# One MoE transformer layer on one core: slots of an expert's block spread over the DMA engines, and no GpSimd drain at the end

## What is computed

```python
scores = sigmoid(t @ w_router); biased = scores + router_bias        # 64 experts
idx = top 8 experts out of the best 4 of 8 groups                    # per token
wsel = scores[idx] / sum(scores[idx]) * 2.5
routed[token] = sum over its 8 experts e of wsel * swiglu(t, wg[e], wu[e], wd[e])
swiglu(t, wg, wu, wd) = (silu(t @ wg) * (t @ wu)) @ wd               # 1024 -> 256 -> 1024
x = x + g2 * (routed + shared)
```

## Time and profile before

| | us |
|---|---|
| median of 3 runs | 1282.87 (1282.39 to 1285.67) |
| the profiled execution | 1285.91 |
| its span, first to last instruction | 1284.1 |
| PE busy | 1203.1 (94%) |
| DVE busy | 462.0 (36%) |
| ACT busy | 197.6 (15%) |
| POOL busy | 193.3 (15%) |

### The profile page before, as it was taken

How to read it: one execution, slowest core, us unless ns; L and a number is a source line. 1 busy time by engine, 2 the same in 40 slices (tenths; PEclk the granted TensorE clock), 3 DMA queues, 4 the chain that set the end, 5 groups by cost and what they waited for, 6 DMA issues and landing times.

```text
span 1284.1 us, 14047 instructions
## 1 busy us (share of the span) xinstructions
PE 1203.1 (94%) x4705; PEld 606.4 (47%) x4705; DVE 462.0 (36%) x1239; ACT 197.6 (15%) x452; POOL 193.3 (15%) x221
## 2 busy tenths in 40 slices
PE   6999999999999999998899998889999898999985
PEld 3444544444888544444444444333444343444442
DVE  2536557100666222555233323222323232233322
ACT  4110001011665001120001100000100010011100
POOL 0000000000221000100022323222222112223212
PEclk9999999999999999998899999988999899999998
DMA  8966661112100302167789999999999999989952
GB/s 275 368 217 229 219 231 65 66 65 83 50 0 1 131 1 106 72 256 290 278 294 364 383 386 378 382 364 375 370 300 379 386 363 391 384 291 381 358 135 35
DMA packets 88910, 311.52 MB, mean 243 GB/s; under 512 B 12400, under 2 KB 38160, under 8 KB 64912
## 3 DMA queue, kind: packets, MB, share of 16 engines
q1 hardware_dynamic: 72480, 272.77, 55.0%
q0 software_dynamic: 14784, 35.68, 11.8%
q10 hardware_dynamic: 1584, 2.27, 0.5%
HBM read 295.47 MB, written 34.08 MB: 257 GB/s over the span
## 4 chain that ended last, share of the span: by engine, by line
PE 80%; DMA 14%; DVE 2%; issue 1%; SPq 1%; ACT 1%; POOL 0%; DVEq 0%; POOLq 0%; ACTq 0%
PE PS L1718 21%; PE PS L1429 19%; PE PS L1739 11%; DMA R_HSA<-w_up_e 5%; DMA R_Z<-w_up_e 5%; PE PS L1597 4%; PE PS L1568 4%; PE PS L1704 3%; PE PS L1501 3%; PE PS L1477 2%; PE PS L1412 2%; DMA out<-second_sum 2%; DMA R_G<-h_rows,gidx 2%; PE PS L1607 2%; PE PS L1489 1%
## 5 line engine op out<-in xcount | busy, mean ns | idle before, releaser
L1429 PE MATMUL PS<-R_WT,R_HSA 128*128 128x512 f32 x576 | 248.2, 592 | 0.0
L1429 PEld LDWEIGHTS PS<-R_WT,R_HSA 128*128 128x128 f32 x576 | 109.3, 190 | 135.9 <-issue 135.8
L1265 DVE TENSOR_TENSOR R_G<-R_G,PS 128x256 f32<-128x256 f32 x50 | 30.4, 608 | 356.6 <-ACT R_G L864 356.6
L1718 PE MATMUL PS<-R_Z,R_G 128*64 128x512 f32 (+1 forms) x384 | 137.5, 603 | 13.0 <-DMA R_XM<-w_up_e 9.7
L1718 PE MATMUL PS<-R_WT,R_G 128*64 128x512 f32 (+1 forms) x352 | 129.1, 636 | 18.9 <-DMA R_WT<-w_up_e 10.9
L657 POOL DMA_INDIRECT R_G<-h_rows,gidx x54 | 56.3, 1042 | 431.6 <-DVE gidx L1254 370.5
L869 ACT ACTIVATE R_G<-PS 128x256 f32<-128x256 f32 x50 | 19.2, 383 | 556.2 <-PE PS L1726 556.2
L1286 DVE SCALAR_TENSOR_TENSOR R_G<-PS,slx,R_XM 128x512 f32<-128x512 f32 x100 | 74.9, 750 | 64.5 <-PE PS L1739 64.5
L1718 PEld LDWEIGHTS PS<-R_Z,R_G 128*64 128x64 f32 (+1 forms) x384 | 52.6, 161 | 92.9 <-issue 92.9
L1718 PE MATMUL PS<-R_XM,R_G 128*128 128x512 f32 (+1 forms) x192 | 88.0, 613 | 0.0
L1718 PEld LDWEIGHTS PS<-R_WT,R_G 128*64 128x64 f32 (+1 forms) x352 | 46.2, 163 | 84.7 <-issue 84.7
(11 more groups left out here) (256 smaller groups left out, 1318.6 us busy)
## 6 DMA issues: line engine op xcount, KB each, us to landing
R_Z<-w_gate_e SPq DMA_DIRECT2D x22, 1024.0 KB, 17.2
R_Z<-w_up_e SPq DMA_DIRECT2D x22, 1024.0 KB, 27.7
R_Z<-w_down_e SPq DMA_DIRECT2D x22, 1024.0 KB, 24.9
R_WT<-w_gate_e SPq DMA_DIRECT2D x21, 1024.0 KB, 16.6
R_WT<-w_up_e SPq DMA_DIRECT2D x21, 1024.0 KB, 30.1
R_WT<-w_down_e SPq DMA_DIRECT2D x21, 1024.0 KB, 27.1
R_WT<-ada_w SPq DMA_DIRECT2D x18, 1024.0 KB, 7.5
R_WT<-w_in SPq DMA_DIRECT2D x9, 2048.0 KB, 10.3
```

What stands on the lines that cost most here:

```text
L1265: dve.tensor_tensor(AR[:, b, :].rearrange("p (k d) -> p d k", k=2), by_line(SIL[:, b, :], 2), by_line(PS[:, b, F:2 * F], 2), ALU.mult).the ...
L1429: ins = mm(PS[:, t, :], HT[:, k, P * t:P * t + P], WR[:, b, k, :], start=k == 0, stop=k == KD - 1)
L1718: ins = mm(PS[w * h:w * h + w, b, :].rearrange("p (g n) -> p g n", g=2), XT[:, b, k, w * h:w * h + w], WGU[n][:, k], start=k == 0, stop=k ...
```

## The change

- `spread_slots(rows, turned)` numbers the slots anew: the partitions of a transfer are taken as 16 runs of rows/16, and neighbouring slots lie on different runs: slots 1 to 16 are the first partition of each run, 17 to 32 the second, and so on; turned, it goes through the runs from the last to the first. There are tables for 128, 96 and 64 rows, in both directions.
- Wide and narrow blocks use them turned at every other block; in a pair block the second expert is turned.
- The tables for 128 and 96 rows are a new input `slots` (128 x 448 float32, 224 KiB), loaded at the head of the shared weights' transfers; TensorE's wait counts one transfer more, and VectorE gets a wait for it ahead of the first `onehot`. For 64 rows the place of `C_SLOT` is used.
- In narrow blocks `onehot` compares 96 slots instead of 128.
- The block is opened with `no_gpsimd_drain=True`: GpSimd's drain at the end is left out.

```diff
+def spread_slots(rows, turned):
+    row = np.arange(rows)
+    engine = row // (rows // 16)
+    return row % (rows // 16) * 16 + (15 - engine if turned else engine) + 1
...
-    c[:, C_SLOT:C_SLOT + P] = f + 1
+    slots = np.zeros((P, S_N), np.float32)
+    for turned in range(2):
+        c[:, C_SLOT + P // 2 * turned:C_SLOT + P // 2 * turned + P // 2] = spread_slots(P // 2, turned)
+        slots[:, S_WIDE[turned]:S_WIDE[turned] + P] = spread_slots(P, turned)
+        slots[:, S_NARROW[turned]:S_NARROW[turned] + NARROW] = spread_slots(NARROW, turned)
...
+        SLOTS = R_T[:, 4096:4096 + S_N]
...
-        block = st.enter_context(nc.Block())
+        block = st.enter_context(nc.Block(no_gpsimd_drain=True))
...
+        def turned(j, b):
+            return (j - PAIRS[j]) % 2 if isinstance(j, int) and j < NM else b
...
             sp.wait_ge(s_u, 8)
+            sp.dma_start(SLOTS, a["slots"]).then_inc(s_ws, 16)
             sp.dma_start(R_W[:, 6144:6656], a["w_router"].rearrange("(p k) n -> p (k n)", p=P)).then_inc(s_ws, 16)
...
-                    dve.tensor_tensor(AH[:, b], bc(cst[:, C_SLOT:C_SLOT + P].unsqueeze(1), [P, NT, P]),
+                    n = rows(j)
+                    at = (S_WIDE if n == P else S_NARROW)[turned(j, b)]
+                    dve.tensor_tensor(AH[:, b, :, 0:n], bc(SLOTS[:, at:at + n].unsqueeze(1), [P, NT, n]),
...
-                                      bc(cst[:, C_SLOT:C_SLOT + h].unsqueeze(1).unsqueeze(1), [P, NT, 2, h]),
+                                      bc(cst[:, C_SLOT:C_SLOT + P].rearrange("p (c s) -> p c s", c=2).unsqueeze(1),
+                                         [P, NT, 2, h]),
...
+            dve.wait_ge(s_ws, 80)
             onehot(0, 0)
...
-            pe.wait_ge(s_ws, 64)
+            pe.wait_ge(s_ws, 80)
```

More of the change, by code:

```diff
@@ L123 @@
 C_N = C_SEL + HA
+S_WIDE = (0, P)
+S_NARROW = (2 * P, 2 * P + NARROW)
+S_N = 2 * P + 2 * NARROW
+def spread_slots(rows, turned):
+    row = np.arange(rows)
+    engine = row // (rows // 16)
+    return row % (rows // 16) * 16 + (15 - engine if turned else engine) + 1
 def constants():
@@ L157, in constants @@
     causal[:, S - P:] = np.where(f > p, NEG, 0.0)
-    return c, causal
+    return c, causal, slots
 def build(nc, a):
@@ L1222, in onehot @@
                 if len(cols) == 1:
-                    dve.tensor_tensor(AH[:, b], bc(cst[:, C_SLOT:C_SLOT + P].unsqueeze(1), [P, NT, P]),
+                    n = rows(j)
+                    at = (S_WIDE if n == P else S_NARROW)[turned(j, b)]
+                    dve.tensor_tensor(AH[:, b, :, 0:n], bc(SLOTS[:, at:at + n].unsqueeze(1), [P, NT, n]),
                                       bc(PM[:, bass.ds(cols[0], 1), :].rearrange("p o t -> p (o t)").unsqueeze(2),
-                                         [P, NT, P]), ALU.is_equal).then_inc(s_ah, 1)
+                                         [P, NT, n]), ALU.is_equal).then_inc(s_ah, 1)
                 else:
@@ L1801 @@
         give(name, array if name == "c" else array.reshape(array.shape[1:]))
-    for name, array in zip(("consts", "causal"), constants()):
+    for name, array in zip(("consts", "causal", "slots"), constants()):
         give(name, array)
```

## The result

| | before | after |
|---|---|---|
| median, us | 1284.27 (1280.37 to 1289.3, 6 runs) | 1276.72 (1273.09 to 1281.64, 6 runs) |
| profiled execution, its span | 1285.91, 1284.1 | 1281.64, 1279.8 |
| second comparison | 1285.12 (17 runs) | 1272.67 (1269.41 to 1276.35, 6 runs) |

The ratio is 0.9939, 95% interval 0.9918 to 0.9960, and in the second comparison 0.9906 (0.9877 to 0.9934). The change makes the kernel 0.6 to 0.9% faster, 8 to 12 us where 42 were forecast.

The account below looks back on a forecast made before the run. TensorE's work with holes left by DMAs, chiefly late up weights, was taken to bound the kernel. Savings of 27.7 + 6.1 + 1.6 + 6.3 = 41.7 us against the median of 1282.9 gave 1241 us, range 1230 to 1262.

Parts of the forecast that it names:

- What bounds the kernel: TensorE's work with holes left by DMAs; eight waits for `w_up_e` of 32.0 us, paced by weights plus the fullest engine's rows.
- the second group: Four TensorE waits for `w_up_e`, 1008.5 to 1092.4 us, ahead of pair blocks; the first group's four stand at 802.6 to 892.2.
- rival C: In transfers of 128 an engine owns two runs of four partitions, 32 apart; 1249.6 us; chance 0.09.
- The slack of 17 us: Supply deficit in each stretch of alternating wide and pair blocks taken as absorbed by the ring of six weight buffers.
- Part 1: Spread rows shorten up-weight waits in both stretches of wide and pair blocks: 12.8 and 14.9 us, sum 27.7.
- Part 2: Kernel's end: the join of the sums lands earlier, removing a gather wait, 6.1 us; the last two scatters save 1.6.
- Part 3: GpSimd's drain at the exit, with nothing running beside it, goes: 6.3 us saved, bounds 0 and 6.3.
- The signs that it named: `w_up_e` waits fall from 32 us to 5 to 15, up-weight landing below 30.1, join below 22, drain row gone.
- rival A: The DMA engines are all full, so levelling frees nothing; only last scatters and drain count: 1275 us; chance 0.10.
- Part 4: Added table load, VectorE's new wait and shorter compare: covered by other work, cost 0; without cover 0.8 us.
- B: At the program's end, the drain's wait is paid elsewhere, unseen: 1247.5 us; chance 0.11.
- D: Engines take rows in turn, partition p on engine p mod 16, so new slots are less level: 1293 us; chance 0.04.

Follow-up runs that it names:

- second comparison: The changed kernel itself, unaltered, timed again beside other kernels on one chip; 1272.67 us, ratio 0.9906 to the kernel before.
- The levelled kernel: Changed kernel with slots of 128 and 64 rows renumbered by the measured partition owners, neighbouring slots on different engines; 1247.87 us, ratio 0.9704.
- the one with a single full engine: The levelled kernel with one engine filled first in every transfer, later slots dealt evenly to the other fifteen; 1283.29 us, ratio 0.9974.
- The spread alone: Changed kernel with GpSimd's drain at the end kept, so new slots only, timed twice; 1279.47 and 1279.12 us, ratios 0.9951 and 0.9949.
- the levelled kernel with the drain: The levelled kernel with GpSimd's drain at the exit put back; 1255.68 us, ratio 0.9767.
- the drain's own comparisons: Kernel before without GpSimd's drain, twice: 1278.06 and 1279.08 us (0.9938, 0.9950); also the levelled kernel with the drain put back: 1255.68 us against 1247.87.
- the 5.91 us of {0 to 3, 32 to 35}: Kernel without the layer, issuing 30 lone indirect DMAs with chosen rows; a 128-row scatter using these partitions took 5.91 us, partitions 0 to 7 took 4.41.

## Why the prediction was wrong

The time is 1276.7 (ratio 0.9939 to the kernel before), forecast was 1241 with a range of 1230 to 1262. Point by point:

**What bounds the kernel: right.** The supply of weights through the fullest engine sets the waits, though not that engine's rows alone. The levelled kernel shows it from one side, the one with a single full engine from the other.

**The step that failed: "Take an engine to own a run of 8 (of 128), 6 (of 96) or 4 (of 64) partitions, as the change's own table assumes."** It holds for 96 alone. All that follows from it is off: the rows of the fullest engine are not 735 before and 537 after but 679 and 610, so 69 instead of 198 were taken away. The prediction had a row that spoke against it. It worked out 29.5 us a period for the second group, where 28.4 and 28.7 were measured, and counted three hits of four. The hits were weaker than they looked. The first group's waits stand at the pair blocks of the wide ranks 12 to 15, and from rank 14 on the wide blocks are narrow, so that two of its three periods have 28 rows by the assumption and not 32: 30.5, 29.5 and 29.5 us, where 30.5, 30.8 and 28.3 were measured. And rival C was dismissed with "the periods above fit both", but with C's own count of 25.0 rows a period the second group comes to 28.7 us, nearer than 29.5. By the measured map the fullest engine has 30.7 and 22.5 rows a period in the two stretches, which gives 21.9 + 8.3 = 30.2 and 21.9 + 6.1 = 28.0 us; measured on average 29.9 and 28.0. The map that was not assumed fits both groups.

The slack of 17 us, on which both savings of Part 1 rest, hung on the same map. With 28.0 us a period the second stretch falls short of TensorE's 23.5 by 27 us, of which 18.9 showed, so 8 were absorbed and not 17; in the first it is 14. That "both give the same 17" was a coincidence.

**Part 1, the spread: 27.7 forecast, about none of it came in the waits** (32.0 us before, 31.8 after). The price of a period did hold where the slots are level: 23.5 and 17.7 rows give 28.2 and 26.7 us, measured on average 28.2 and 27.1. It was too low for the change, where it gives 29.5 and 27.4, and 30.2 and 28.1 were measured (29.8 and 28.2 in the second profile). That is the second error, in size: a row was priced as if it cost the same whether one engine or eight carry it. With it, even the right count would have promised too much: rival C's price, 0.14 us of stall a row, gives 69 x 0.14 = 10 us. The spread alone gave 6 in all.

**Part 2, the tail.** The last scatters: right. The one on the chain took 4.8 us instead of 5.8; the last one lands 4.9 us after its start at 1274.6, before 5.8 (it started at 1271.8 and the drain of the earlier trace rows at 1277.6). Together 1.9 us, forecast 1.6. (In its working the forecast took two rows less in each. The last two experts have 67 and 63 tokens, so it is one row and two, 0.8 to 1.8 us by its own price.) The join: wrong. It was to come below 22 us and took 25.8 (24.6 in the second profile of the same kernel), and the wait behind it stayed, 3.2 us of 4.3 (1.9 in the second profile). It needed level engines, as the prediction said. In the levelled kernel with the drain it takes 23.8 us, the scatter behind it starts 24.8 us after the join's issue, and 0.4 us of the wait are left; in the one without the drain that scatter starts after 23.2 us, and the wait is gone.

**Part 3, the drain: right.** 6.3 us forecast. Its row is gone, the span ends with the last landing, and alone it measures 6 to 8 us in three comparisons.

**The signs that it named.** The waits stayed and the landing times did not fall either (30.7 us, before 30.1), so it was neither the forecast's picture nor rival A's.

**Part 4, what is added:** nothing of it appears among TensorE's waits.

**The rivals.** A (all engines full) falls with the levelled kernel: the same bytes, at a share no lower than before, took 37 us less. Its number, 1275, is what was measured, for another reason; a rival that gives the right time is not thereby the cause. B (the drain paid elsewhere) falls with the drain's own comparisons. C (two runs of four, 32 apart) named the owner that was measured in transfers of 128. It was worked out with 705 and 567 rows since it left the 64-row scatters at runs of four, and its 1249.6 us is as wrong as the forecast. It had got 0.09, though it was a rule written down, against an assumption that stood only in the table of the change itself. D (rows in turn) falls with the 5.91 us of {0 to 3, 32 to 35}.

The forecast of 1241 was in effect one for a levelled kernel: 0.9704 of 1282.9 is 1244.9 us. What was wrong is that this change was taken to be that kernel.

## What to carry to other kernels

A DMA is as late as its fullest engine, so rows that are dealt out unevenly slow down everything behind them in that engine; here a numbering of slots alone moved the time by 43 us of 1285. Measure who owns which partition, for each number of rows separately, with lone transfers that use a few chosen rows: it takes 30 DMAs and 170 us, and a table that is taken on trust can be right for one size and wrong for the next. And when a model of the pace misses one of two groups, count it as evidence against the assumption in which the groups differ.

## What the runs showed of the hardware beyond that

- The owner of a partition depends on the number of rows of the indirect DMA: two runs of four 32 apart (128), a run of six (96), two pairs 32 apart (64).
- Alone, an accumulating scatter without a row takes 2.70 us, with 8 rows on one engine 5.91, so 0.40 us a row. A gather with 8 on one engine takes 4.02, against 2.1 for the shortest of the kernel before, which gives an estimate of 0.24 us a row. A row is 4 KB in both.
- Neither the mean DMA share nor the rate of a window of 60 us tells such kernels apart. The share was 0.99 to 1.02 in kernels whose time differs by 3%. The rate was 387 and 392 GB/s in the levelled kernel, but 392 and 386 also in the one with one full engine, which is 35 us slower.
- A part of the gain of levelling was the clock. In the two profiles from the same chip, 6.0 of 21.3 us are the same matmuls at a mean granted clock of 0.987 instead of 0.981.
